# Layer-norm variance as [128 tokens, 4] columns in the last stage, with the reciprocal root spread over the partitions by four transposes

## What is computed

```python
def _layernorm(x, g, b):
    mu = jnp.mean(xf, axis=-1, keepdims=True)
    xc = xf - mu
    y = xc * lax.rsqrt(jnp.mean(xc * xc, axis=-1, keepdims=True) + EPS)
    return (y * g + b)
u = jax.nn.silu(_layernorm(_depthwise_conv(u, dw_w, dw_b), ln_g, ln_b))
x_new = x + gate * ((u * jax.nn.silu(gz)) @ w_out)
return _rmsnorm(x_new, final_norm_g)
```

## Time and profile before

| What | us |
|---|---|
| median of 3 runs | 4270.45 |
| lowest and highest | 4269.01, 4273.16 |
| span of the profiled execution | 4268.6 |
| TensorE busy | 3642.0 (85%) |
| VectorE busy | 2855.7 (67%) |
| ScalarE busy | 1513.0 (35%) |
| GpSimd busy | 359.5 (8%) |

### The profile page before, as it was taken

The page is one execution under the profiler, slowest core; times in us unless marked ns, Lnnn a source line. Parts: engine busy times, 40 slices in busy tenths (PEclk is TensorE's granted clock), DMA queues, the critical chain, the costliest instruction groups (busy, mean ns, idle before and its releaser), DMA issues. The chain is left out here.

```text
span 4268.6 us, 52411 instructions
## 1 busy us (share of the span) xinstructions
PE 3642.0 (85%) x17412; PEld 2905.4 (68%) x17412; DVE 2855.7 (67%) x4163; ACT 1513.0 (35%) x2842; POOL 359.5 (8%) x272
## 2 busy tenths in 40 slices
PE   5799969999989999489987998985899886749898
PEld 1678746777768888368866877764677775636666
DVE  6667668999910101175632179996999998868994
ACT  0343347777733323122214222213222213124553
POOL 3000060000000000000000000000000000422332
PEclk8899989999999999789998999997999998979999
DMA  7344355333222211346522213104131121143332
GB/s 275 107 119 130 99 170 97 107 111 106 86 79 81 84 66 64 122 164 217 201 96 99 82 55 109 64 35 144 65 109 65 64 78 61 60 147 117 145 137 99
DMA packets 291990, 460.86 MB, mean 108 GB/s; under 512 B 35331, under 2 KB 172291, under 8 KB 289797
## 3 DMA queue, kind: packets, MB, share of 16 engines
q1 hardware_dynamic: 267938, 420.78, 28.8%
q0 software_dynamic: 10720, 37.24, 3.2%
q10 hardware_dynamic: 13188, 0.99, 0.2%
HBM read 309.35 MB, written 149.59 MB: 108 GB/s over the span
## 5 line engine op out<-in xcount | busy, mean ns | idle before, releaser
L1046 DVE SCALAR_TENSOR_TENSOR s5b_cacc<-s5b_cu,conv_w,s5b_cacc 128x1024 f32<-128x1024 f32 x480 | 576.7, 1278 | 0.0
L160 PE MATMUL s_out_ps<-s_w_hi,s_y_hi 128*128 128x512 f32 x1024 | 420.5, 411 | 24.2 <-DVE s_y_lo L2060 21.6
L161 PE MATMUL s_out_ps<-s_w_lo,s_y_hi 128*128 128x512 f32 x1024 | 408.4, 399 | 0.0
L162 PE MATMUL s_out_ps<-s_w_hi,s_y_lo 128*128 128x512 f32 x1024 | 408.4, 399 | 0.0
L160 PE MATMUL s5b_out_ps<-s5b_xT_hi,s5b_w_hi 128*128 128x512 f32 x768 | 312.5, 407 | 62.2 <-DVE s5b_xT_lo L1267 62.2
L1046 DVE SCALAR_TENSOR_TENSOR s5a_cacc<-s5a_cu,conv_w,s5a_cacc 128x1024 f32<-128x1024 f32 x300 | 360.2, 1268 | 0.0
L1267 DVE TENSOR_TENSOR s_xT_lo<-s_xT,s_xT_hi 128x512 fp32r<-128x512 f32 x64 | 43.6, 692 | 466.6 <-ACT s_xT_hi L1226 466.6
L160 PE MATMUL s5a_out_ps<-s5a_xT_hi,s5a_w_hi 128*128 128x512 f32 x768 | 309.1, 403 | 36.6 <-DVE s5a_xT_lo L1267 36.6
L160 PE MATMUL s_out_ps<-s_xT_hi,ug_w_hi 128*128 128x512 f32 x768 | 305.6, 398 | 0.0
L162 PE MATMUL s5b_out_ps<-s5b_xT_hi,s5b_w_lo 128*128 128x512 f32 x768 | 305.2, 397 | 0.0
L161 PE MATMUL s5b_out_ps<-s5b_xT_lo,s5b_w_hi 128*128 128x512 f32 x768 | 304.8, 397 | 0.0
(11 more groups left out here) (225 smaller groups left out, 7810.2 us busy)
## 6 DMA issues: line engine op xcount, KB each, us to landing
s_k_in<-kT_d SPq DMA_DIRECT2D x32, 768.0 KB, 5.9
qT_d<-s_qk_t SPq DMA_DIRECT2D x34, 512.0 KB, 3.3
s_x<-in_x SPq DMA_DIRECT2D x16, 1024.0 KB, 6.3
s_q_in<-qT_d SPq DMA_DIRECT2D x32, 512.0 KB, 4.2
s_x<-in_x SPq DMA_DIRECT2D x32, 512.0 KB, 5.2
gT_d<-s_g_sb SPq DMA_DIRECT2D x64, 256.0 KB, 2.0
s_y<-gT_d SPq DMA_DIRECT2D x8, 2048.0 KB, 9.0
s_xr<-in_x SPq DMA_DIRECT2D x32, 512.0 KB, 4.7
```

What stands on the lines that cost most here:

```text
L160: pe.matmul(acc, lh, rh, start=first, stop=False)
L161: pe.matmul(acc, lh, rl, start=False, stop=False)
L162: return pe.matmul(acc, ll, rh, start=False, stop=last)
L1046: dve.scalar_tensor_tensor(acc, u, w, acc, ALU.mult, ALU.add).then_inc(self.step, 1)
```

## The change

The variance matmul swaps its operands. The sum of squares of 128 tokens is now the loaded side, and one column of `averager` is the moving one, so that the variance of a token comes out on the partition of that token: four matmuls fill the four columns of a [128, 4] tile. The 15 instructions of the root work on this tile. Then TensorE transposes each column, read with step 0 as a [128, 128] operand, into 128 columns of a new PSUM tile `rstd_ps` [128, 512], which holds the root of each token on every partition as before. `scale` reads that tile. TensorE does the spread of chunk n + 1 in body n, in s = 0 after k = 4, and at the head after mean(1). The variance of chunk 1 moves from s = 1 to s = 0, after k = 0. The root no longer waits for the scales of the chunk before (`z_ready`) but for the spread of it, the spread waits for those, and the first scale of a chunk waits for its spread.

```diff
--- before.py
+++ after.py
@@ -1773,9 +1773,9 @@
             ch_sum = sb("ch_sum", [P, CW])
             sq = sb("sq", [P, 4, CW])
             sq_sum = sb("sq_sum", [P, CW])
-            ln_var = sb("ln_var", [P, CW])
-            ln_rstd = sb("ln_rstd", [P, CW])
-            ln_tmp = sb("ln_tmp", [P, CW])
+            ln_var = sb("ln_var", [P, TPC])
+            ln_rstd = sb("ln_rstd", [P, TPC])
+            ln_tmp = sb("ln_tmp", [P, TPC])
             y_hi = sb("y_hi", [P, KT, CW], F32R)
             y_lo = sb("y_lo", [P, KT, CW], F32R)
             xr = sb("xr", [P, 2, TPC, D])
@@ -1786,7 +1786,8 @@
             fin_tmp = sb("fin_tmp", [P, TPC])
             out_ps = ps("out_ps", [P, 2, 2, 512])
             mean_ps = ps("mean_ps", [P, CW])
-            var_ps = ps("var_ps", [P, CW])
+            var_ps = ps("var_ps", [P, TPC])
+            rstd_ps = ps("rstd_ps", [P, CW])
             fixed_loaded = sem("fixed_loaded")
             averager_made = sem("averager_made")
             z_loaded = [sem(f"z_loaded{i}") for i in range(2)]
@@ -1799,6 +1800,7 @@
             sq_step = sem("sq_step")
             var_ready = sem("var_ready")
             rs_step = sem("rs_step")
+            rstd_spread = sem("rstd_spread")
             z_ready = sem("z_ready")
             sg_ready = sem("sg_ready")
             ln_ready = sem("ln_ready")
@@ -1913,7 +1915,17 @@
                     pe.wait_ge(sq_step, (n + 1) * SUMS)
                     if before >= 1:
                         pe.wait_ge(rs_step, (n - 1) * (RSQRT_STEPS + 1) + 1)
-                    pe.matmul(var_ps[:], averager[:], sq_sum[:], start=True, stop=True).then_inc(var_ready, 1)
+                    for s in range(TPC):
+                        ins = pe.matmul(var_ps[:, s:s + 1], sq_sum[:, s * P:(s + 1) * P], averager[:, 0:1], start=True, stop=True)
+                    ins.then_inc(var_ready, 1)
+
+                def spread(n, before):
+                    pe.wait_ge(rs_step, (n + 1) * (RSQRT_STEPS + 1))
+                    if before >= 1:
+                        pe.wait_ge(z_ready, n * KT)
+                    for s in range(TPC):
+                        ins = pe.transpose(rstd_ps[:, s * P:(s + 1) * P], ln_rstd[:, s:s + 1].to_broadcast([P, P]), ident[:])
+                    ins.then_inc(rstd_spread, 1)
 
                 pe.wait_ge(averager_made, 1)
 
@@ -1922,6 +1934,7 @@
                         mean(0, 0)
                         variance(0, 0)
                         mean(1, 1)
+                        spread(0, 0)
                     for s in range(TPC):
                         if before * TPC + s >= 2:
                             pe.wait_ge(x2_ready, n * TPC + s - 1)
@@ -1935,8 +1948,10 @@
                                 ins.then_inc(y_used, 1)
                             elif k == KT - 1:
                                 ins.then_inc(out_ready, 1)
-                            if before == 0 and s == 1 and k == 0:
+                            if before == 0 and s == 0 and k == 0:
                                 variance(1, 1)
+                            if after >= 1 and s == 0 and k == KT // 2:
+                                spread(n + 1, before + 1)
                             if after >= 2 and s == TPC - 1 and k == KT - 2:
                                 variance(n + 2, before + 2)
 
@@ -2040,15 +2055,17 @@
                 def normalise(n, slot, before):
                     dve.wait_ge(var_ready, n + 1)
                     if before >= 1:
-                        dve.wait_ge(z_ready, n * KT)
+                        dve.wait_ge(rstd_spread, n)
                     dve.tensor_scalar(ln_var[:], var_ps[:], EPS, None, ALU.add).then_inc(rs_step, 1)
                     step = n * (RSQRT_STEPS + 1) + 1
                     dve.wait_ge(rs_step, step)
                     rsqrt(dve, rs_step, step, ln_rstd[:], ln_var[:], ln_tmp[:])
 
                 def scale(n, slot, k):
+                    if k == 0:
+                        dve.wait_ge(rstd_spread, n + 1)
                     dve.wait_ge(sq_ready, n * KT + k + 1)
-                    dve.tensor_tensor(z[:, slot, k, :], z[:, slot, k, :], ln_rstd[:], ALU.mult).then_inc(z_ready, 1)
+                    dve.tensor_tensor(z[:, slot, k, :], z[:, slot, k, :], rstd_ps[:], ALU.mult).then_inc(z_ready, 1)
 
                 def gate_y(n, slot, k):
                     dve.wait_ge(sg_ready, n * KT + k + 1)
```

## The result

| | before | after |
|---|---|---|
| median, lowest to highest, 18 runs each, us | 4272.91, 4268.26 to 4276.84 | 4265.67, 4257.62 to 4270.14 |
| ratio with its 95% interval | | 0.9982 [0.9976, 0.9989] |
| span of the profiled execution | 4268.6 | 4258.4 |
| TensorE's variance(0) in it, the first use of the new code | 3802.94 | 3801.91 |
| from there to the end, **the stage** | 465.7 | 456.5 |

The changed kernel is 7.2 us faster by the medians, 0.18%; the forecast was 3.2 us slower. The last line of the table is the one to compare profiles by: up to variance(0) the two kernels do the same work, and in the profiles of this study variance(0) starts anywhere between 3797.84 and 3807.45 us (e3 aside, which shortens GpSimd's first sums), so a span carries up to 10 us that the earlier stages made. The stage got 9.2 us shorter; of the 10.2 between the spans 1.0 lay before it.

A forecast was written before the change was run, and what follows sets the result against it. VectorE's chain, its root held by GpSimd's additions, bounds the loop: 20.3 + 7.45 + 29.4 = 57.2 us against 55.3. With the head 7.2 us ahead the sum is 4270.45 + 3.2 = 4273.6, range 4260 to 4284.

The forecast's parts named there:

- What bounds the kernel: In the last stage VectorE is busy 9 tenths or more; TensorE is not the bound, waiting 26.9 us for GpSimd's sums.
- G to C: From the end of the last y and z product to the start of GpSimd's first addition: 10.17 us.
- C to R: From the start of GpSimd's first addition to the root's end: 10.1 us, one small instruction held per addition.
- rival (b): Two small root instructions get in per GpSimd gap: 2.4 us less per loop, time 4264; chance 0.15.
- R to S: From the root's end to TensorE's product end for tokens 0 to 127: 0.44 + 4.2 + 2.5 + 0.3 = 7.45 us.
- S to G: From TensorE's product end for tokens 0 to 127 to the last y and z product's end: 29.4 us, unchanged.
- Sum: Head, loops of 57.2 us and tail together: +3.2 us on the span of 4268.6.
- Head: TensorE idles nearly 14 us before variance(1); body 1's last y and z product ends at 3927.4, 7.2 us ahead.
- Rival (a): The root's small instructions escape GpSimd's hold: 48.1 us per loop, time 4237; chance 0.08.
- Rival (c): TensorE's clock stays low through all 18 products after the root: 9.0 us in place of 7.45, time 4280; chance 0.20.
- The rule on the shared pair: Between VectorE and GpSimd in SBUF, whichever starts first holds the shared pair for its whole instruction, small ones included.
- the last rival: Set up after the result, before the experiments: VectorE's work costs the time; no size or chance given.

The follow-up runs named there:

- e3: GpSimd makes one of its seven channel additions per chunk, against the changed kernel: 4228.12 us, ratio 0.9900.
- the wide roots: The root on [128, 64] and on [128, 128] tiles instead of [128, 4], against the changed kernel: 4277.38 and 4284.55 us.
- e1: Spread of the next chunk behind the last product of s = 0 instead of behind k = 4, against the changed kernel: 4240.29 us, ratio 0.9930.

## Why the prediction was wrong

- **What bounds the kernel, and G to C**: right. Nothing in front of the root moved (9.4 us from G to its start; G to C 10.1 in the mean for 10.17). The old root is given as 16.3 us up to the residual at 3960.54; that is 16.5, and nothing is built on it.
- **C to R, the step that failed.** "I take one small instruction per GpSimd addition too": there are two. The mean of C to R is 7.6 us, not 10.1, 2.5 less in each of four bodies, 9.9 us. Five or six instructions are held in a body, where seven were forecast. The prediction's rows 7 and 8 showed only that a single short instruction can be held, and could not show what a queue of them does. The prediction had the case as rival (b), with C to R at 7.7 and the loop 2.4 shorter; its grounds (the gap between two of GpSimd's additions, the next instruction 0.2 us behind) are what the trace shows. It was given 0.15 because the long root of before let in one per addition, and the wide roots show that this is a matter of length: evidence from [128, 512] instructions did not carry to those of 0.16 us. Its 4264 is 1.7 us from the median of 4265.67.
- **R to S**: too long by 0.6 us in the mean (6.85 for 7.45), 2.4 us in all. The clock was low for 2.9 to 5.0 us behind R, which is 2.0 us of full-speed work in the mean and not 2.5; with that figure the sum gives 0.44 + 4.2 + 2.0 + 0.3 = 6.9.
- **S to G**: right, 29.4.
- **Sum**: forecast span 4271.8, measured 4258.4, 13.4 less. C to R has 9.9 of them and R to S 2.4; G to C and the rounding up of the loop to 57.2 have 0.3 each, and the stretch from the last of these G to the end, 115.0 for 115.6, has 0.6. The first G was 0.1 late.
- **Head**: right to 1.1 us. Idle before variance(1) 13.45 us for "nearly 14". G of body 1 came at 3927.52 for 3927.4, but that is luck: the stage had begun 1.0 us early, and behind variance(0) it is 125.6 for 124.5. Of this 0.8 is TensorE's wait for the root in body 1, forecast as "no wait of weight".
- **Rival (a)**, no hold: wrong for the change. e3, with one addition left, shows its price: a period of 47.85 where (a) said 48.1. Its time is 4228 and not 4237, but 9.5 us of that lie ahead of the stage.
- **Rival (c)**, the clock: wrong. R to S never exceeded 7.32 us in bodies 2 to 5. The low clock lasts 2.9, 3.6, 5.0 and 4.7 us from R on. In the kernel before, from the start of the mean's matmul, which ended the waits there, it is (1 - 0.78) x 8 / 0.5 = 3.5 us in body 2, and by these stretches 5.4, 6.1 and 5.9 in the next three:

```profile
4012.12:4020.12 8.00, 8.00 (x22) 5.74 (x23) 7.03 (x23) 1.15 (x2) 0.00 (x0) 0.66 0.00 0
4066.09:4074.09 8.00, 8.00 (x21) 5.64 (x22) 7.25 (x18) 1.15 (x2) 0.00 (x0) 0.62 0.00 0
4120.81:4128.81 8.00, 8.00 (x21) 5.67 (x22) 7.29 (x18) 1.73 (x4) 0.00 (x0) 0.63 0.00 0
```

  The Trainium skill's rule in "TensorE: Matmul & The Clock Gate", Part 4, that transposes do not count for the clock, shows no cost here: the low stretches that hold the transposes are no longer than the others. No run puts other matmuls in the transposes' place, so the rule itself is not decided.
- **The rule on the shared pair**, which the prediction drew from "SBUF — State Buffer" of the Trainium skill, "SBUF: two separate sides": the trace agrees with the hold (1.1 to 1.3 us) and with its condition, that the one that starts first has the ports. How many get in between two of GpSimd's instructions follows from the rows alone.

What the forecast saw rightly is why 45.7 us less work on VectorE bring so little: the wait changes its place from the mean, with nothing urgent behind it, to the transposes, with the residual's products behind it. e1 shows what that place costs, 22 us of stage; it could have been named as a cure before. VectorE's work itself, the last rival, is not what sets the time: with VectorE's work unchanged the place alone gave 22 us.

## What to carry to other kernels

Before putting a wait into an in-order queue, list what stands behind it and who needs that first; a wait moved behind the last product that another engine needs was worth 22 us of stage here, the whole change 9. Short instructions of VectorE from SBUF to SBUF beside a queue of such additions of GpSimd (1.3 us each) are held once for each addition: count them by pairs up to 0.18 us of own length, and singly, for the most part, from 0.20 on. Undo a loss at the head only after the loop behind it has no slack wait left: the same edit was worth 0 us on the change and 7 on the version with the late spread.

## What was not expected of the hardware

- The pairing, and its edge: [128, 4] and [128, 16] at 0.15 to 0.18 us go in pairs, [128, 64] at 0.20 to 0.23 mostly singly, [128, 128] at 0.23 to 0.29 singly. The starts explain it: the second of a pair starts some 0.02 us ahead of GpSimd's next addition. Held instructions end 0.02 to 0.03 us behind the addition on [128, 4] and 0.05 to 0.08 on [128, 64], and the next comes too late. Why they end later is not shown.
- GpSimd pays little for it: its additions stand 1.35 us apart under the small root (8.08 for six) and 1.32 with nothing beside them; under the old root it was 1.58 (9.49 for six).
- C to R alternates between two values, 6.95 and 8.30, by whether five or three of the fifteen run ahead of GpSimd's first addition; one addition, 1.35 us, is the step between them.
- Stages in front of an edit that never changed shift its start by up to 10 us between profiles (3797.84 to 3807.45).
